# High parts of twenty weight slabs brought by rounding transfers, with a re-ordered first stage, in a two-layer decoder step on one core

## What is computed

```python
y = gelu(x @ w_y + b_y)                      # 1024 x 1024 weights
u = x @ w_x + b_x                            # 1024 x 1024
xc = conv_b + sum(conv_w[k] * upad[:, k:k + T] for k in range(4))
r  = sigmoid(blocks(xc) @ w_ga + b_ga)       # 8 blocks of 128 x 128
gi = sigmoid(blocks(xc) @ w_gi + b_gi)
h  = scan(a, mult * gi * xc)                 # a, mult from r, along the tokens
out = (h * y) @ w_out + b_out                # 1024 x 1024
x = layer_norm(ALPHA * x + out)
```

## Time and profile before

| | |
|---|---|
| median of three runs (lowest, highest) | 1053.46 us (1053.33, 1054.89) |
| the profiled execution, its own time | 1053.91 us |
| its span, first to last instruction | 1052.0 us |
| TensorE busy | 1035.5 us (98%), 8237 matmuls |
| VectorE / ScalarE / GpSimd busy | 840.5 / 660.8 / 227.1 us |
| TensorE's granted clock, mean | 0.996 of full speed |
| HBM read | 135.95 MB |

### The profile page before, as it was taken

How to read it: one execution, slowest core, us unless ns; L and a number is a source line. 1 busy time by engine, 2 the same in 40 slices (tenths; PEclk the granted TensorE clock), 3 DMA queues, 4 the chain that set the end, 5 groups by cost and what they waited for, 6 DMA issues and landing times.

```text
span 1052.0 us, 20682 instructions
## 1 busy us (share of the span) xinstructions
PE 1035.5 (98%) x8237; PEld 1017.5 (97%) x8237; DVE 840.5 (80%) x1283; ACT 660.8 (63%) x1159; POOL 227.1 (22%) x285
## 2 busy tenths in 40 slices
PE   8999999999999999999999999999999999999995
PEld 8999999999999999999999888999999999999995
DVE  6999898879678697796874574888879697696776
ACT  5999858665746557463766785675836647457333
POOL 2111032011111111103234574310111111111023
PEclk9999999999999999999999999999999999999998
DMA  7323213467877877866042121164777877878402
GB/s 257 122 90 101 81 61 129 113 152 161 176 174 155 198 167 164 194 167 206 21 141 68 41 67 36 41 181 81 160 171 157 200 160 159 205 161 178 137 2 85
DMA packets 54479, 139.83 MB, mean 133 GB/s; under 512 B 5632, under 2 KB 21440, under 8 KB 54368
## 3 DMA queue, kind: packets, MB, share of 16 engines
q0 software_dynamic: 14512, 53.60, 29.3%
q1 hardware_dynamic: 39584, 84.32, 24.2%
q10 hardware_dynamic: 288, 0.59, 0.2%
HBM read 135.95 MB, written 3.56 MB: 133 GB/s over the span
## 4 chain that ended last, share of the span: by engine, by line
PE 88%; POOL 3%; ACT 3%; DVE 3%; issue 2%; DMA 1%; SPq 0%; DVEq 0%; POOLq 0%; ACTq 0%
PE bank L2488 8%; PE bank L2507 8%; PE bank L2490 8%; PE bank L2509 8%; PE bank L2489 8%; PE bank L2508 8%; PE bank L2233 8%; PE bank L2234 7%; PE bank L2235 7%; PE bank L2320 3%; PE bank L2321 3%; PE bank L2322 3%; PE bank L2461 1%; PE bank L2463 1%; PE bank L2462 1%
## 5 line engine op out<-in xcount | busy, mean ns | idle before, releaser
L851 ACT ACTIVATE w_hi<-stage 128x1024 fp32r<-128x1024 f32 x164 | 168.2, 1053 | 124.9 <-DMA stage<-w_up 71.6
L1374 DVE TENSOR_TENSOR w_lo<-stage,w_hi 128x1024 fp32r<-128x1024 f32 x164 | 197.3, 1222 | 53.9 <-ACT w_hi L851 53.9
L2507 PE MATMUL bank<-part_hi,w_hi 128*128 128x272 f32 x672 | 194.8, 290 | 0.5 <-issue 0.5
L2509 PE MATMUL bank<-part_hi,w_lo 128*128 128x272 f32 x672 | 194.0, 289 | 0.0
L2508 PE MATMUL bank<-part_lo,w_hi 128*128 128x272 f32 x672 | 193.4, 288 | 0.0
L2233 PE MATMUL bank<-x_hi,w_hi 128*128 128x288 f32 (+1 forms) x480 | 140.0, 292 | 1.2 <-DVE w_lo L1368 1.1
L2234 PE MATMUL bank<-x_lo,w_hi 128*128 128x288 f32 (+1 forms) x480 | 138.7, 289 | 0.0
L2235 PE MATMUL bank<-x_hi,w_lo 128*128 128x288 f32 (+1 forms) x480 | 138.0, 288 | 0.0
L2507 PEld LDWEIGHTS bank<-part_hi,w_hi 128*128 128x128 f32 x672 | 126.5, 188 | 1.7 <-issue 0.8
L2509 PEld LDWEIGHTS bank<-part_hi,w_lo 128*128 128x128 f32 x672 | 126.7, 188 | 0.0
L2508 PEld LDWEIGHTS bank<-part_lo,w_hi 128*128 128x128 f32 x672 | 126.7, 188 | 0.0
(11 more groups left out here) (298 smaller groups left out, 2931.6 us busy)
## 6 DMA issues: line engine op xcount, KB each, us to landing
stage<-w_up SPq DMA_DIRECT2D x54, 512.0 KB, 3.7
stage<-w_down SPq DMA_DIRECT2D x52, 512.0 KB, 4.0
stage<-w_down POOLq DMA_DIRECT2D x48, 512.0 KB, 5.4
stage<-w_up POOLq DMA_DIRECT2D x44, 512.0 KB, 5.5
stage<-w_qkv SPq DMA_DIRECT2D x10, 512.0 KB, 4.4
stage<-w_x SPq DMA_DIRECT2D x8, 512.0 KB, 5.4
stage<-w_y SPq DMA_DIRECT2D x8, 512.0 KB, 3.5
stage<-w_out SPq DMA_DIRECT2D x8, 512.0 KB, 3.3
```

Source lines behind the costliest of these rows:

```text
L851: A(w_hi[:, slot_of(l, k), :], raw_of(l, c, k), ACT.Copy).then_inc(s_whi, 1)
L1374: vt.tensor_tensor(w_lo[:, s, :], raw_of(l, c, k), w_hi[:, s, :].bitcast(F32), ALU.subtract)\
L2507: mm(out, wh, xh[:, k, :], start=(fresh and k == 0), stop=False, skip_group_check=True)
L2509: ins = mm(out, wl, xh[:, k, :], start=False, stop=(k == 1), skip_group_check=True)
```

## The change

Five parts. (1) Slabs 4 to 23 of the recurrent block (`cast_in`) are no longer rounded by ScalarE: GpSimd issues a transfer that reads the slab from HBM a second time and writes it, converted to float32r, into its `w_hi` slot. The plain load into `stage` remains, for the low part. GpSimd's twenty transfers stand in its program in five groups of four: after six residual tiles, after the next two, in steps 3 and 5 behind their two residual tiles each, and at the end. A transfer waits until its slot is free and until the low part of slab `w - 4` is made; VectorE's split waits for both transfers of its slab. ScalarE's split skips these slabs, and `hi_count` corrects the counts. (2) The first packet of vectors is issued after slab 0's rounding instead of before. (3) Slab 1 is loaded, rounded and subtracted in two halves, with quarter 3 of x between them. (4) The first two y tiles are made k by k. (5) `w_x` and `w_y` are laid out on the host in slabs (`pair_tiles`), so that a row of a slab is 4 KB in one piece; before it was four pieces of 1 KB.

```diff
@@ SyncE, start
             load_x(0)
-            load(0, xv[:, 0:4, 0:256])
+            load(0, w_x[0])
             for k in (1, 2):
                 load_x(k)
-            load(1, xv[:, 4:8, 0:256])
-            load_x(3)
-            load_pair(("pair", 0), yv, 0, 2)
+            for k in (4, 6):
+                at = 256 * (k - 4)
+                sp.dma_start(stage[:, where[1][0], at:at + 512], w_x[1][:, at:at + 512])\
+                    .then_inc(s_marrived if k == 4 else s_arrived[where[1][0]], 16)
+                if k == 4:
+                    load_x(3)
+            load_tiles(0, w_y, 2)
@@ ScalarE, split
+                    if kind == "w" and cast_in(w):
+                        continue
@@ VectorE, split
-                    dve.wait_ge(s_whi, j + 1)
+                    kind, w = jobs[j]
+                    if kind == "w" and cast_in(w):
+                        dve.wait_ge(s_arrived[where[j][0]], where[j][1])
+                        dve.wait_ge(s_cast[w % 4], 16 * (w // 4))
+                    else:
+                        dve.wait_ge(s_whi, hi_count(j))
                     vt.tensor_tensor(lo, raw, hi.bitcast(F32), ALU.subtract).then_inc(s_wlo, 1)
@@ GpSimd
+            def cast_slab(w):
+                if w >= 8:
+                    pool.wait_ge(*free_at[w - SLOTS])
+                    pool.wait_ge(s_wlo, slab_job[w - 4] + 1)
+                dst = w_hi[:, w % SLOTS, :]
+                if w < 16:
+                    view = (w_y if w % 4 > 1 else w_x)[2 * (w // 4) + w % 2]
+                else:
+                    view = quad(ov, w // 4 - 4, w % 4)
+                    dst = dst.rearrange("p (k c) -> p k c", k=2)
+                pt.dma_start(dst, view).then_inc(s_cast[w % 4], 16)
+            pool.wait_ge(s_xb, 32)
+            for w in range(4, 8):
+                cast_slab(w)
...
             pool.wait_ge(s_xchi, 2)
             residual0(0, range(6, 8))
+            for w in range(8, 12):
+                cast_slab(w)
             for s in range(2, 6):
                 pool.wait_ge(s_xchi, s + 1)
                 residual0(1, range(2 * s - 4, 2 * s - 2))
+                if s in (3, 5):
+                    for w in range(4 * (s // 2) + 8, 4 * (s // 2) + 12):
+                        cast_slab(w)
+            for w in range(20, 24):
+                cast_slab(w)
@@ TensorE, step 0
                     group_by_k(range(2), 0, pieces0,
-                               lambda k: ((s_xlo, k // 2 + 1), (s_wlo, k // 4 + 1)))
+                               lambda k: ((s_xlo, k // 2 + 1), (s_mlo, 1) if k in (4, 5) else (s_wlo, k // 4 + 1)))
...
+                if s == 0:
...
+                    group_by_k(range(mark[("y", 0)], mark[("y", 0)] + 2), 0, pieces1, lambda k: ((s_wlo, j + 3 + k // 4),))
+                    continue
                 pe.wait_ge(s_wlo, j + 4)
```

More of the change, by code:

```diff
@@ L246, in build @@
         s_whi, s_wlo = sem("slab_hi_done"), sem("slab_lo_done")
+        s_cast = [sem(f"slab_hi_arrived_{k}") for k in range(4)]
+        s_marrived = sem("half_of_second_slab_arrived")
+        s_mhi, s_mlo = sem("half_of_second_slab_hi_done"), sem("half_of_second_slab_lo_done")
         s_unit = sem("unit_done")
@@ L409, in read_by @@
             return sum(1 for r in reader[:n] if r == who)
-        yv, xv, ov, qv, pv = (w.rearrange("(k p) c -> p k c", p=128) for w in (w_y, w_x, w_out, w_qkv, w_o))
+        ov, qv, pv = (w.rearrange("(k p) c -> p k c", p=128) for w in (w_out, w_qkv, w_o))
         def quad(view, g, j):
@@ L610, in build, with cast_in, hi_count @@
             frees(("qkv", g), qkv_unit(g, 1, n - 1) + 1, n)
+        def cast_in(w):
+            return 4 <= w < 24
+        slab_job = {job[1]: j for j, job in enumerate(jobs) if job is not None and job[0] == "w" and job[1] < 24}
+        def hi_count(j):
+            return j + 1 - sum(1 for w, k in slab_job.items() if cast_in(w) and k <= j)
         def next_jobs(s):
@@ L697, in load_pair, with load_tiles @@
                     load(job_at[name][0] + jj + k, view[:, 4 * k:4 * k + 4, c:c + 256])
+            def load_tiles(p, w, jj):
+                for k in range(2):
+                    load(job_at[("pair", p)][0] + jj + k, w[2 * p + k])
             def load_quad(name, view, g):
@@ L772, in _ @@
                 else:
-                    load_pair(("pair", p), xv, 256 * p)
-                    load_pair(("pair", p), yv, 256 * p, 2)
+                    load_tiles(p, w_x, 0)
+                    load_tiles(p, w_y, 2)
                 j = job_at[("gates", p)][0]
@@ L877, in _ @@
             late = VEC["sinks"][0]
+            split([0])
             act.dma_start(vecs[:, 0:late], vec[:, 0:late]).then_inc(s_vec, 16)
-            split([0])
             x_split(0, [1, 2])
-            split([1])
+            st, count = where[1]
+            act.wait_ge(s_marrived, 16)
+            A(w_hi[:, 1, 0:512], stage[:, st, 0:512], ACT.Copy).then_inc(s_mhi, 1)
             x_split(0, [3])
+            act.wait_ge(s_arrived[st], count)
+            A(w_hi[:, 1, 512:1024], stage[:, st, 512:1024], ACT.Copy).then_inc(s_whi, 1)
             split([2, 3])
@@ L1437, in _ @@
             x_split(0, [1, 2])
-            split([1])
+            raw = stage[:, where[1][0], :]
+            dve.wait_ge(s_mhi, 1)
+            vt.tensor_tensor(w_lo[:, 1, 0:512], raw[:, 0:512], w_hi[:, 1, 0:512].bitcast(F32), ALU.subtract)\
+                .then_inc(s_mlo, 1)
             x_split(0, [3])
+            dve.wait_ge(s_whi, 2)
+            vt.tensor_tensor(w_lo[:, 1, 512:1024], raw[:, 512:1024], w_hi[:, 1, 512:1024].bitcast(F32), ALU.subtract)\
+                .then_inc(s_wlo, 1)
             split([2, 3])
@@ L2191, in slab_lo @@
                 hi, lo, raw = split_targets(j)
-                pool.wait_ge(s_whi, j + 1)
+                pool.wait_ge(s_whi, hi_count(j))
                 pool.wait_ge(s_wlo, j)
@@ L2363, in _, with pieces1 @@
                     gates(s - 1)
+                if s == 0:
+                    def pieces1(t):
+                        return [(*slab(w0 + 2, k // 4, 256 * (k % 4) + 128 * t), *act_cols(x_hi, x_lo, k, 0))
+                                for k in range(KT)]
+                    group_by_k(range(mark[("y", 0)], mark[("y", 0)] + 2), 0, pieces1, lambda k: ((s_wlo, j + 3 + k // 4),))
+                    continue
                 pe.wait_ge(s_wlo, j + 4)
@@ L2852, with pair_tiles @@
     down_tiles = down_tiles.reshape(2 * CHUNKS * 4, 128, 1024)
+    def pair_tiles(w):
+        return w.reshape(2, 4, 128, 4, 256).transpose(3, 0, 2, 1, 4).reshape(8, 128, 1024)
     arrays = {
         "xp_t": x_prompt[0].T, "xs_t": x_sample.reshape(NS, D).T, "vec": vec,
-        "w_y": lru_w_y[0], "w_x": lru_w_x[0], "w_ga": lru_w_ga[0], "w_gi": lru_w_gi[0], "w_out": lru_w_out[0],
+        "w_y": pair_tiles(lru_w_y[0]), "w_x": pair_tiles(lru_w_x[0]), "w_ga": lru_w_ga[0], "w_gi": lru_w_gi[0], "w_out": lru_w_out[0],
         "w_qkv": swa_w_qkv[0][:, cols], "w_o": swa_w_o[0][q_cols], "w_up": up_tiles, "w_down": down_tiles,
```

4 lines of the change are left out of this document (2 added, 2 removed).

## The result

The changed kernel takes 1057.20 us in the median (7 runs, 1056.04 to 1059.39); the kernel before took 1053.68 us beside it (7 runs, 1053.20 to 1055.29). The ratio is 1.0038, 95% interval 1.0029 to 1.0047: slower by 3.5 to 4 us, where 1051.7 was forecast. It is the side of rival (b). The profiled execution took 1056.41 us, with a span of 1054.4.

A forecast was written before the change was run, and what follows sets the result against it. TensorE, busy for 1035.5 of 1052.0 us, was taken as the bound, so only its waits could be gained. 1.8 - 0.3 + 0.6 = 2.1 us from 1053.91 gave 1051.8; median forecast 1051.7, range 1049.9 to 1054.0.

The forecast's parts named there:

- rival (b): Recurrent block: late transfers make VectorE the bound; at 7 us issue to landing, 2.5 us of loss, time 1056.4; chance 0.14.
- The first product may come up to 0.3 us sooner: Kernel start, first product at 7.70 us: up to 0.3 us sooner through the new layout; nothing counted for it.
- The second step begins 1.8 us earlier, bounds 1.0 and 2.15: TensorE's second step, at 21.45 us before: 1.0 us lead from the x low-part chain plus 0.8 for faster transfers.
- the 0.8 us for the layout: First slabs' loads: 4-KB rows instead of 1-KB rows speed the transfers, counted as 0.8 us of the second step's lead.
- I take L = 4.7: Rounding transfers' time from issue to landing, L, taken as 4.7 us; waits of 1.5 us at slab 8, 0.8 at slab 12.
- Each us on L costs 2 us there: Step 6: each us of transfer landing time L delays VectorE's low part 2 us; it comes at 84.6 + 2L.
- gains 1.0 us in each root wait passed: Recurrences: with roundings off ScalarE, VectorE no longer waits for the root, 3.8 us in four recurrences, 1.0 each.
- case (c): Full start won, nothing lost: 3.1 us gained, 1050.8, at most 1050.0; needs transfer landing time below 4.4 us; chance 0.17.
- keeps a lead of 1.5: Step 6: TensorE, 1.8 us early, waits 0.3 us for VectorE's low part and keeps 1.5 us of lead.
- The waits at slab 16 fall where the gate products have more slack: Recurrent block, third late group: waits for slab 16's transfer fall where gate products have more slack; no loss summed for them.
- the wait of 0.57 us: Behind the block: TensorE's wait on GpSimd's sum of squares should go, gaining 0.6 us, bounds 0 and 0.6.
- The sum: Whole kernel: 1.8 at the start, less 0.3 at step 6, plus 0.6 behind the block, 2.1 us gained.

The follow-up runs named there:

- transfers ahead: Changed kernel with GpSimd's transfers of slabs 8 to 19 issued before the step's two residual tiles instead of behind them: 1052.95 us, ratio 1.0000 to before.
- transfers alone: Changed kernel's rounding transfers and slab layout, with the first slabs in the order of the kernel before: 1057.78 us, ratio 1.0035 to before.
- free high parts: Changed kernel's new start, with high parts of slabs 8 to 23 neither rounded nor brought (output not the reference's): 1052.33 us, ratio 0.9992 to before.
- start alone: Changed kernel without rounding transfers, ScalarE rounding all slabs; new start and 4-KB rows stay: 1052.96 us, ratio 0.9995 to before.
- longer warm-up: Split in the root wait, plus two more products of ones before the first product (WARM 13 to 15): 1052.57 us, ratio 0.9987 to before.
- second slab first: Changed kernel with the second slab's transfer ahead of the first's in the groups of slabs 8, 12 and 16: 1060.14 us, ratio 1.0065 to before.
- split in the root wait: Transfers ahead, with VectorE's one split of steps 2, 4 and 6 put before the recurrence instead of behind it: 1051.97 us, ratio 0.9986 to before.
- old rows: Start alone, but with w_x and w_y in 1-KB rows as in the kernel before: 1053.21 us, ratio 1.0003 to before.

## Why the prediction was wrong

- "**The first product may come up to 0.3 us sooner**", "**I count nothing**": it came at 8.37. In fourteen traces slab 0's rounding starts between 5.20 and 5.91 us: 5.24 to 5.47 in the five without transfers, 5.20 to 5.91 in the nine with them (ahead 5.29, transfers alone 5.89). No rounding transfer is issued before 16 us, so this looks like scatter from run to run; one trace of each kernel doesn't show it.
- "**The second step begins 1.8 us earlier, bounds 1.0 and 2.15**": 1.38, inside the bounds. The binding event was named rightly (a wait on x's low part shows in most variants); the 0.8 us for the layout was mis-sized, 0.3 to 0.5 in the one pair of traces that separates it.
- "**I take L = 4.7**": mis-sized, and this is the largest part of the error: 0.3 us were set down for late landings, and they cost 0.38%, 4.0 us (changed kernel against transfers ahead). The first slab of each group took 4.4, 5.9 and 5.9 us to its use, and slab 23 7.0. Over all twenty, issue to landing was 4.3 at least, 7.1 in the median and 9.2 at most: four 512-KB transfers that are issued 0.55 to 0.7 us apart share the queue. I had bounded a group's first transfer with single ones.
- "**Each us on L costs 2 us there**", "VectorE's low part comes at 84.6 + 2L": right. With 4.4 and 5.9 it gives 94.9; measured 95.63, 0.7 later. Part of that is the lead that VectorE brings: it is ready for slab 8 at 42.83 us, 0.33 ahead of the 43.16 before, not 0.8. At step 4, 66.6 was predicted and 66.65 measured, but by luck: that lead was 0.5 us too large and the wait at slab 8, 1.05 for 1.5 us, as much too long.
- VectorE "**gains 1.0 us in each root wait passed**": wrong as a gain, and this is the step that fails even with every transfer on time. The root wait only absorbs what VectorE lost at the slab; when nothing is lost it stays, because the serial chain on ScalarE sets it. So a landing in time was not enough for case (c), and even the 2.1 us that I summed did not come: with everything on time the change gives 1.0000 (transfers ahead), with free high parts 0.9992.
- TensorE "**keeps a lead of 1.5**" fails even without late transfers. The recurrence's period was 27.6 us before the change against TensorE's 27.1, so VectorE loses 0.5 us on each pair and reaches its last low product just in time. Moving TensorE earlier makes that product late: 0.54 us at 126.9 in the start alone. The trace before showed no wait there, and I took this for slack; the slack in the earlier trace rows falling from 1.5 to 1.0 us from pair to pair said otherwise.
- "**The waits at slab 16 fall where the gate products have more slack**": wrong. The gate products do, but other readers don't: that group alone costs 1.3 us. Its path is VectorE's low product, then ScalarE's reading of y (`z`, L969), then the bank that `w_out`'s second tile pair needs.
- Behind the block, "**the wait of 0.57 us**" on the sum of squares should go. It stayed, 0.71, since VectorE now waited 1.94 us for slab 23: its transfer was forecast to be issued near 126 us and to land near 131, and was issued at 129.30 and landed at 136.2. The wait goes where slab 23 is late by 0.7 us at most (transfers ahead 0.66, longer warm-up 0.28).
- **The sum**, by measured terms in the profiled execution: -1.4 at the start, +1.6 by step 6, +2.2 from there to `w_out`'s last group, +0.2 behind it: 2.6, against 2.4 between the spans and 2.5 between the times. Rival (b) had the mechanism, VectorE as the bound through late landings. Its +2.5 for L = 7 is luck: it put all of the loss at step 6, where TensorE was to be 3.1 us late and was 0.18, and nothing at slab 16 and the last group, where 2.2 us were lost. I gave it 0.14, because the adding transfers land in 5.4 us in the median. That median was of transfers in other stages, with other company on the queue.

What stays open: why slab 12's and 16's transfers took 1.5 us longer than slab 8's. The traces hold a candidate. In the changed kernel, in transfers alone and in second slab first, SyncE issued a plain load of 512 KB 0.9 us ahead of the group's first transfer at slabs 12 and 16, which then took 4.6 to 5.9 us to land, and 1.7 us ahead at slab 8, which took 4.3 to 4.4. With the transfers ahead, no plain load was issued in the 2.7 us before, and they took 3.9 to 4.7. No run changes this alone, and none separates the load on the queue from anything in GpSimd; issuing took 0.53 to 0.78 us each in every kernel, beside a busy VectorE or an idle one.

## What to carry to other kernels

A wait that a serial chain sets is a place to put work, not time that comes back when other work on the same engine is removed: here roundings off ScalarE gave nothing that could be measured, and one 1.2-us subtraction moved into the wait brought the kernel to 1.4 in a thousand under before, once the transfers had freed it from ScalarE's order. When a copy is handed from an engine to a queue, price it from where its issue stands in the issuing engine's program to the landing of the first of a group under its own sisters' load, and put the issue ahead of work that nobody waits for. And compare the periods of the two engines, not only their slack at one point: a lead given to the faster one is eaten by the slower at each round.

## What the runs showed of the hardware

- Two residual tiles of GpSimd took 2.98 us at 36.54 us in the changed kernel, beside VectorE's splits, and 1.47 at 39.27 with the transfers ahead, beside its recurrence. With the split moved (split in the root wait), the next pair, of 128x288 tiles, took 3.19 us beside it at 48.71; with the split in its old place it took 1.65 at 49.20 (transfers ahead). VectorE pays too: its split took 1.45 us beside the tiles (64.53 in the changed kernel) and 1.22 without (64.48 with transfers ahead). The Trainium skill, page "SBUF — State Buffer", section "SBUF: two separate sides", says that a VectorE operation with two inputs in SBUF and a GpSimd operation that reads SBUF share a port pair, of which the first holds it and the other blocks. The direction agrees: the split has two such inputs. The rule alone does not give the sizes, since the recurrence's instructions have two such inputs as well, and the pair beside them took 1.47.
- TensorE's clock fell in two of fourteen profiles (old rows, split in the root wait). TensorE had then been idle for 2.07 and 1.83 us before its first product; the granted clock was 0.50, the 1.2-GHz level, from 8 to 11 us. With 0.54 to 1.81 us of idle time it stayed at 1.00, and one execution with 1.81 is too near for idle time alone to be called the cause. The idle time differs since the 26 passes of the warm-up took between 4.80 us (in both of these) and 5.92 from run to run. Such an execution reaches the second step up to 0.6 us later, which the wait on x's low part otherwise hides.
- A rounding transfer of 512 KB never landed before 3.6 us from its issue, and took up to 9.4 beside its sisters.
